# The second block of tokens lies mirrored up to the merge, so that one score matmul a level serves both blocks

## The reference

```
S_t = diag(exp(log_a_t)) S_{t-1} + k_t^T v_t
o_t = q_t S_t
# over a block, with b = cumsum(log_a) along the tokens:
scores[t, s] = sum_c q[t, c] k[s, c] exp(b[t, c] - b[s, c])   for s <= t, else 0
o = scores @ v + (q * exp(b)) @ S_before
```

## Time and profile before

| | us |
|---|---|
| median of 3 runs | 1714.46 (1712.81 to 1714.52) |
| the profiled execution | 1714.55 |
| its span, first to last instruction | 1712.8 |
| TensorE busy / weight loads | 1688.7 / 1683.3 |
| VectorE busy | 1093.8 |
| ScalarE busy | 802.7 |
| GpSimd busy | 200.8 |

### The profile page before, as it was taken

How to read it: one execution, slowest core, us unless ns; L and a number is a source line. 1 busy time by engine, 2 the same in 40 slices (tenths; PEclk the granted TensorE clock), 3 DMA queues, 4 the chain that set the end, 5 groups by cost and what they waited for, 6 DMA issues and landing times.

```text
span 1712.8 us, 37004 instructions
## 1 busy us (share of the span) xinstructions
PE 1688.7 (99%) x13836; PEld 1683.3 (98%) x13836; DVE 1093.8 (64%) x1744; ACT 802.7 (47%) x1058; POOL 200.8 (12%) x170
## 2 busy tenths in 40 slices
PE   7999999999999999999998999999999999999999
PEld 7999999999999999999998999999999999999999
DVE  6547548888888885665596544554455445555675
ACT  6575335455465444543464433543345334443453
POOL 4000001222111110005430000000000000025200
PEclk9999999999999998999998999999999999999999
DMA  9455656565665555675563555555555555555564
GB/s 261 147 195 175 219 187 199 181 200 166 186 209 189 179 175 176 225 271 186 168 193 121 190 183 173 183 192 176 181 173 185 187 181 172 179 189 184 167 191 148
DMA packets 162545, 318.66 MB, mean 186 GB/s; under 512 B 11700, under 2 KB 96436, under 8 KB 162500
## 3 DMA queue, kind: packets, MB, share of 16 engines
q1 hardware_dynamic: 160196, 315.91, 57.7%
q10 hardware_dynamic: 2304, 2.16, 0.4%
HBM read 299.94 MB, written 18.09 MB: 186 GB/s over the span
## 4 chain that ended last, share of the span: by engine, by line
PE 94%; DVE 2%; issue 2%; ACT 1%; DMA 1%; SPq 0%; POOL 0%; ACTq 0%; DVEq 0%; POOLq 0%
PE bank L291 27%; PE bank L292 26%; PE bank L293 26%; PE bank L309 3%; PE bank L311 3%; PE bank L310 3%; PE bank L583 2%; PE bank L570 1%; PE bank L559 1%; ACT whi L274 0%; DVE wlo L279 0%; PE bank L601 0%; DMA v_st<-v_spill 0%; PE bank L581 0%; PE bank L615 0%
## 5 line engine op out<-in xcount | busy, mean ns | idle before, releaser
L274 ACT CAST whi<-raw 128x1024 fp32r<-128x1024 f32 x534 | 548.3, 1048 | 469.2 <-PE bank L293 362.1
L279 DVE TENSOR_TENSOR wlo<-raw,whi 128x1024 fp32r<-128x1024 f32 x534 | 650.1, 1248 | 150.2 <-ACT whi L274 149.6
L291 PE MATMUL bank<-a_hi,whi 128*128 128x264 f32 x2576 | 737.8, 286 | 0.0
L292 PE MATMUL bank<-a_lo,whi 128*128 128x264 f32 x2576 | 730.9, 284 | 0.0
L293 PE MATMUL bank<-a_hi,wlo 128*128 128x264 f32 x2576 | 730.4, 284 | 0.0
L292 PEld LDWEIGHTS bank<-a_lo,whi 128*128 128x128 f32 x2576 | 486.7, 189 | 0.1
L291 PEld LDWEIGHTS bank<-a_hi,whi 128*128 128x128 f32 x2576 | 486.2, 189 | 0.4 <-issue 0.3
L293 PEld LDWEIGHTS bank<-a_hi,wlo 128*128 128x128 f32 x2576 | 484.1, 188 | 0.0
L291 PE MATMUL bank<-b_hi,whi 128*128 128x264 f32 x1280 | 365.4, 285 | 8.8 <-DVE wlo L279 6.7
L292 PE MATMUL bank<-b_lo,whi 128*128 128x264 f32 x1280 | 364.4, 285 | 0.0
L293 PE MATMUL bank<-b_hi,wlo 128*128 128x264 f32 x1280 | 364.2, 285 | 0.0
(11 more groups left out here) (168 smaller groups left out, 1571.5 us busy)
## 6 DMA issues: line engine op xcount, KB each, us to landing
raw<-in_stream SPq DMA_DIRECT2D x534, 512.0 KB, 4.3
m_spill<-stage SPq DMA_DIRECT2D x32, 132.0 KB, 4.7
lev<-m_spill SPq DMA_DIRECT2D x16, 264.0 KB, 5.4
S<-in_state_hgrn SPq DMA_DIRECT2D x16, 256.0 KB, 5.1
out_new_hgrn_sample<-S SPq DMA_DIRECT2D x16, 256.0 KB, 4.5
S<-in_state_gla SPq DMA_DIRECT2D x8, 512.0 KB, 7.5
out_new_gla_sample<-S SPq DMA_DIRECT2D x8, 512.0 KB, 5.6
room<-in_x SPq DMA_DIRECT2D x7, 528.0 KB, 8.0
```

Source lines behind the costliest of these rows:

```text
L274: act.copy(whi[:, s, :], raw[:, s, :]).then_inc(hi_ready, 1)
L279: dve.tensor_tensor(wlo[:, s, :], raw[:, s, :], whi[:, s, :].bitcast(F32), ALU.subtract).then_inc(lo_ready, 1)
L291: pe.matmul(out, whi[:, s, w], hi[:, k0 + k, :], start=start and k == 0, stop=False)
L292: pe.matmul(out, whi[:, s, w], lo[:, k0 + k, :], start=False, stop=False)
```

## The change

The second block's tokens (columns 128 to 255) are stored in reverse order from the very first operand on, and put back when the two branches are merged. `MIRROR` lists the three column ranges as (to, of) pairs, the middle one reversed. `a_hi` and `a_lo` are now made by three instructions each, as are the norm's reciprocal and the merge's add.

In the mirrored block a later token stands left of an earlier one. Level 0 aside, a level's query runs are the right runs of the first block and the left runs of the second, and its key runs the other way round. So 64 query columns of the one block and 64 of the other fill the 128 columns of one matmul, and 64 keys of each fill the 128 columns of `k_lev`, which needs no zeros; cells where a query of one block meets a key of the other are thrown away by the new mask `both`. GpSimd builds `both` from `masks` and `ident` with 14 copies after the start. `cells` describes such a pattern: two blocks, runs at a pitch, and the run's columns.

The sums of the second block run from its far end: a second scan, subtracting, starts at column 129, and column 128 is set to zero by GpSimd. Two small VectorE instructions form two totals a head, which GpSimd copies ahead of `cum` into two more columns of it. `kd` needs a bias for the first block only, so it is two instructions. The masking of the scores is now one instruction for levels 1 to 4 (512 columns) and one for levels 5 to 7 (384 columns).

```diff
...
+MIRROR = [(slice(0, P), slice(0, P)), (slice(P, NP_TOK), slice(NP_TOK - 1, P - 1, -1)),
+          (slice(NP_TOK, TOK), slice(NP_TOK, TOK))]
 def build(nc, t):
...
     masks = sb("masks", [P, CELLS])
+    both = sb("both", [P, LEVELS - 1, P])
     ident = sb("ident", [P, 3 * P])
...
     v_st = sb("v_st", [P, 2, TOK])
-    cum = sb("cum", [P, TOK])
+    cum = sb("cum", [P, TOK + 2])
+    totals = sb("totals", [P, 2, HEADS])
     k_b = sb("k_b", [P, TOK])
...
         pass
-    k_pad = sb("k_pad", [P, LEVELS - 1, NP_TOK])
-    probs = sb("probs", [P, 2, CELLS])
+    k_lev = sb("k_lev", [P, LEVELS - 1, P])
+    probs = sb("probs", [P, LEVELS - 1, P])
     pairs = sb("pairs", [P, 3, P])
...
     silu_done = sem("silu_done")
+    first_zero, total_ready, masks_ready = sem("first_zero"), sem("total_ready"), sem("masks_ready")
     ls_abs, ls_exp, ls_ln = sem("ls_abs"), sem("ls_exp"), sem("ls_ln")
...
-    def tokens(ap, h, side):
-        return ap.rearrange("c (p w j) -> c p w j", w=2, j=h)[:, :, side, :]
+    def cells(ap, h, at, step, pitch):
+        return bass.AP(ap.tensor, ap.offset + at, [list(ap.ap[0]), [step, 2], [pitch, 64 // h], [1, h]])
+    def rights(ap, h):
+        return cells(ap, h, h, P - h, 2 * h)
+    def lefts(ap, h):
+        return cells(ap, h, 0, P + h, 2 * h)
+    def packed(ap, h):
+        return cells(ap, h, 0, 64, h)
+    def mids(ap, h):
+        return bass.AP(ap.tensor, ap.offset + h - 1, [list(ap.ap[0]), [P + 1, 2], [2 * h, 64 // h], [0, h]])
...
                 pe.matmul(DG[:, 2 * B * P:(2 * B + 1) * P], k_b[:, at], q_b[:, at], start=True, stop=True)
-                for l in range(1, LEVELS):
-                    pe.matmul(SC[B][:, (l - 1) * 64:l * 64], k_pad[:, l - 1, at], lev[:, l, 0, B * 64:(B + 1) * 64],
-                              start=True, stop=True)
+            for l in range(1, LEVELS):
+                pe.matmul(SC[(l - 1) // 4][:, (l - 1) % 4 * P:((l - 1) % 4 + 1) * P], k_lev[:, l - 1, :], lev[:, l, 0, :],
+                          start=True, stop=True)
             pe.matmul(DG[:, P:2 * P], lev[:, 0, 1, :], lev[:, 0, 0, :], start=True, stop=True)\
...
                 act.wait_ge(x_landed[list(X_PARTS).index(k)], 16)
-            act.activation(a_hi[:, k, :], x_in[:, k, :], ACT.Identity, scale=gains[:, 0, k:k + 1]).then_inc(a_hi_ready, 1)
+            for to, of in MIRROR:
+                last = act.activation(a_hi[:, k, to], x_in[:, k, of], ACT.Identity, scale=gains[:, 0, k:k + 1])
+            last.then_inc(a_hi_ready, 1)
             round_slab(act, *wide_slab(T_RANK, k), first=k < RING)
...
             act.wait_ge(h_sem["kd_turned"], before(H))
-            act.activation(kd[:], cum[:, 0:NP_TOK], ACT.Exp, scale=-1.0, bias=cum[:, NP_TOK - 1:NP_TOK])\
-               .then_inc(h_sem["kd_exp"], 1)
+            act.activation(kd[:, 0:P], cum[:, 0:P], ACT.Exp, scale=-1.0, bias=cum[:, TOK + 1:TOK + 2])
+            act.activation(kd[:, P:NP_TOK], cum[:, P:NP_TOK], ACT.Exp, scale=-1.0).then_inc(h_sem["kd_exp"], 1)
...
         for k in range(KT):
-            gained_rest(k, a_hi, a_lo, x_in, gains[:, 0, k:k + 1], a_hi_ready, a_lo_ready)
+            dve.wait_ge(a_hi_ready, k + 1)
+            for to, of in MIRROR:
+                last = dve.scalar_tensor_tensor(out=a_lo[:, k, to], in0=x_in[:, k, of], scalar=gains[:, 0, k:k + 1],
+                                                in1=a_hi[:, k, to].bitcast(F32), op0=ALU.mult, op1=ALU.subtract)
+            last.then_inc(a_lo_ready, 1)
             rest_slab(dve, *wide_slab(T_RANK, k))
...
             dve.wait_ge(root_ready, n + 1)
-            dve.reciprocal(r_bc[:], rs[:]).then_inc(r_ready, 1)
+            for to, of in MIRROR:
+                last = dve.reciprocal(r_bc[:, to], rs[:, of])
+            last.then_inc(r_ready, 1)
             dve.wait_ge(r_ready, n + 1)
...
+            one = ones[:, 0:1].to_broadcast([P, P])
             for H in range(first, last):
-                dve.tensor_tensor_scan(gates[:, H, 0:NP_TOK], ones[:, 0:1].to_broadcast([P, NP_TOK]),
-                                       log_gate[:, H, 0:NP_TOK], 0.0, ALU.mult, ALU.add).then_inc(sums_ready, 1)
+                dve.tensor_tensor_scan(gates[:, H, 0:P], one, log_gate[:, H, 0:P], 0.0, ALU.mult, ALU.add)
+                dve.tensor_tensor_scan(gates[:, H, P + 1:NP_TOK], one[:, 1:P], log_gate[:, H, P:NP_TOK - 1], 0.0,
+                                       ALU.mult, ALU.subtract).then_inc(sums_ready, 1)
...
                 sums(8, HEADS)
+                dve.wait_ge(first_zero, 1)
+                dve.wait_ge(sums_ready, HEADS)
+                dve.tensor_tensor(totals[:, 0, :], gates[:, :, NP_TOK - 1], log_gate[:, :, NP_TOK - 1], ALU.subtract)\
+                   .then_inc(total_ready, 1)
+                dve.wait_ge(total_ready, 1)
+                dve.tensor_tensor(totals[:, 1, :], gates[:, :, P - 1], totals[:, 0, :], ALU.subtract).then_inc(total_ready, 1)
         dve.wait_ge(silu_done, 2 + HH)
...
             h = HALF[l]
-            pairs = P // h
-            left, right = tokens(cum[:, 0:NP_TOK], h, 0), tokens(cum[:, 0:NP_TOK], h, 1)
-            mid = left[:, :, h - 1:h].to_broadcast([P, pairs, h])
-            dve.tensor_tensor(lev[:, l, 0, :].rearrange("c (p j) -> c p j", j=h), right, mid, ALU.subtract)
-            return dve.tensor_tensor(lev[:, l, 1, :].rearrange("c (p j) -> c p j", j=h), mid, left, ALU.subtract)
+            if l == 0:
+                dve.tensor_tensor(lev[:, 0, 0, :], cum[:, P:NP_TOK], cum[:, TOK:TOK + 1].to_broadcast([P, P]), ALU.subtract)
+                return dve.tensor_tensor(lev[:, 0, 1, :], cum[:, P - 1:P].to_broadcast([P, P]), cum[:, 0:P], ALU.subtract)
+            dve.tensor_tensor(packed(lev[:, l, 0, :], h), rights(cum[:], h), mids(cum[:], h), ALU.subtract)
+            return dve.tensor_tensor(packed(lev[:, l, 1, :], h), mids(cum[:], h), lefts(cum[:], h), ALU.subtract)
...
         dve.wait_ge(const_landed, 16 * 6)
+        dve.wait_ge(masks_ready, 1)
...
                 h = HALF[l]
-                q, k = tokens(q_b[:, 0:NP_TOK], h, 1), tokens(k_b[:, 0:NP_TOK], h, 0)
-                lq = lev[:, l, 0, :].rearrange("c (p j) -> c p j", j=h)
-                lk = lev[:, l, 1, :].rearrange("c (p j) -> c p j", j=h)
-                dve.tensor_tensor(lq, lq, q, ALU.mult)
-                return dve.tensor_tensor(lk if l == 0 else tokens(k_pad[:, l - 1, :], h, 0), lk, k, ALU.mult)
+                if l == 0:
+                    dve.tensor_tensor(lev[:, 0, 0, :], lev[:, 0, 0, :], q_b[:, P:NP_TOK], ALU.mult)
+                    return dve.tensor_tensor(lev[:, 0, 1, :], lev[:, 0, 1, :], k_b[:, 0:P], ALU.mult)
+                lq, lk = packed(lev[:, l, 0, :], h), packed(lev[:, l, 1, :], h)
+                dve.tensor_tensor(lq, lq, rights(q_b[:], h), ALU.mult)
+                return dve.tensor_tensor(cells(k_lev[:, l - 1, :], h, 0, h, 2 * h), lk, lefts(k_b[:], h), ALU.mult)
...
             dve.wait_ge(h_sem["pv_done"], before(H))
-            for B in range(2):
-                dve.tensor_tensor(probs[:, B, :], SC[B][:, 0:CELLS], masks[:], ALU.mult).then_inc(h_sem["masked"], 1)
+            for n, (first, last) in enumerate(((0, 4), (4, LEVELS - 1))):
+                dve.tensor_tensor(probs[:, first:last, :], SC[n][:, 0:(last - first) * P].rearrange("s (l t) -> s l t", t=P),
+                                  both[:, first:last, :], ALU.mult).then_inc(h_sem["masked"], 1)
...
                 h = HALF[l]
-                to = pairs[:, 0:3:2, :].rearrange("s b (p w j) -> s b p w j", w=2, j=h)[:, :, :, 1, :]
-                cells = probs[:, :, (l - 1) * 64:l * 64].rearrange("s b (p j) -> s b p j", j=h)
+                to = cells(pairs[:, 0, :], h, h, 2 * P - h, 2 * h)
+                of = packed(probs[:, l - 1, :], h)
...
                 dve.wait_ge(h_sem["masked"], (LEVELS + 1) * H + (l + 3))
-                last = dve.tensor_tensor(to, to, cells, ALU.add)
+                last = dve.tensor_tensor(to, to, of, ALU.add)
                 last.then_inc(h_sem["probs_ready" if l == LEVELS - 1 else "masked"], 1)
...
             dve.wait_ge(tiles_drained, T + 1)
-            dve.tensor_tensor(merged[:, m, :], m_in[:, m, 0, :], m_in[:, m, 1, :], ALU.add).then_inc(merge_ready, 1)
+            for to, of in MIRROR:
+                last = dve.tensor_tensor(merged[:, m, of], m_in[:, m, 0, to], m_in[:, m, 1, to], ALU.add)
+            last.then_inc(merge_ready, 1)
...
         pool.memset(eps_col[:], EPS).then_inc(consts_set, 1)
-        pool.memset(s_feat[:], 0.0)
-        pool.memset(k_pad[:], 0.0).then_inc(consts_set, 1)
+        pool.memset(s_feat[:], 0.0).then_inc(consts_set, 1)
...
+        def side_masks(l, side):
+            h = HALF[l]
+            to = both[:, l - 1, side * 64:(side + 1) * 64].rearrange("s (p j) -> s p j", j=h)
+            if h == 1:
+                finer = ident[:, 0:P].rearrange("s (p w) -> s p w", w=2)[:, :, side:side + 1]
+            else:
```

(12 more changed lines are left out.)

## The result

The kernel with the change took 1691.56 us (median of four runs, 1690.76 to 1693.46), the kernel before, beside it, 1714.49 us (four runs, 1712.81 to 1719.91). The ratio is 0.9855, with an interval of 0.9835 to 0.9875. A second comparison, later, gave 1691.12 us (four runs, 1690.65 to 1691.70) against 1715.01 us (seven runs), 0.9853 [0.9833, 0.9873]. The forecast was 1692.2 us, in a range of 1688.5 to 1701.5.

What follows compares the result with a forecast made beforehand. The prediction took TensorE, 94% of the chain, as the bound, with VectorE's loop close behind in D=1 heads. It summed 1714.55 - 19.1 (scores) + 1.8 (D=1 heads) - 5.1 (clock) = 1692.2 us, range 1688.5 to 1701.5.

Steps and rivals of the forecast that it cites:

- The scores: TensorE's score part of each head: 20 passes of 0.110 us, 2.20 us, saving 1.59 us a head, 19.1 us over 12.
- The D=1 heads: HGRN heads, one value tile: 30.56 us each after the change, 0.26 us lost in each of 7 periods, 1.8 us.
- The account of the gaps: VectorE's gaps of 1.00 and 0.63 us in an HGRN head get used up; the loop through three engines needs 30.26 us.
- what is added to it, 0.3 us a head: Extra loop time in HGRN heads from kd's split exponential, a small GpSimd copy, and q_b and k_b copies upon VectorE's adds.
- the upper ends: Largest additions to the HGRN heads' loop, 0.8 us together, if GpSimd and VectorE lock each other out whenever they meet.
- The D=2 heads: GLA heads, two value tiles: the saved 1.59 us counts whole, since the loop goes through TensorE's scores.
- the half microsecond ahead of the scores: In GLA heads TensorE stands still 0.49 us, waiting for VectorE's new states; this wait was to stay.
- the slower rival: New patterns are slower on VectorE, 35 re-laid instructions a head, and the kernel with them: 1727 us; chance 0.06.
- Start, sums, masks, merge: Extra instructions at the start, in scans, GpSimd mask copies and the merge's add: covered by waits or idle time, nothing taken.
- The clock: The granted clock's fall in the last head, costing 5.1 us, no longer happens: -5.1 us.
- the light stretch: Last head's 0.5 us wait, narrow scores, turns and one-column work before the clock falls; 1.59 us shorter after the change.
- the rival's chance: Rival that the granted clock falls once all the same, giving 1697.3 us; chance 0.22.

## Why the prediction was right

*The scores.* Right, step by step. Predicted 2.20 us for the score part of a head, measured 2.23; predicted 1.59 us saved, measured 1.56 in a D=1 head and 1.57 in the period of a D=2 one.

*The D=1 heads.* The account of the gaps was exact but for the first head: the loop was to need 30.26 us, and it needs 30.40 - 0.14 = 30.26. The term that was mis-sized is what is added to it, 0.3 us a head. The rows show next to nothing. kd's exponential is two instructions on ScalarE (L840, L841), which overlap in part and take 0.58 us together for 0.49, less than the 0.14 more that was allowed. The small GpSimd copy took over the long time instead of adding to it, 2.15 and 0.40 us for 2.37. The adds take 2.42 us for 2.35. The mask instructions, of 512 and 384 columns, take 1.14 us for 1.16. By the sum a D=1 head was to take 30.56 us with VectorE as its bound; it takes 30.40, and TensorE is still the bound, except in the first head (30.69). TensorE's own period was put at 30.30; it saved 1.49 of the 1.56 us, the other 0.07 are spread over its matmuls, none as large as 0.05. With the 0.3 us that the first head loses, the seven periods brought 10.1 us where 9.3 were forecast, 0.8 of the 1.4 us by which the forecast fell short in the profiled execution (22.4 for 23.8). Against the median, 1691.56 us, the forecast is off by 0.6 only because that launch was the fastest of the four.

The Trainium skill, "SBUF — State Buffer", section SBUF: two separate sides, has a GpSimd instruction and a VectorE one with two SBUF inputs lock each other out for a whole instruction. The 2.15 us of a copy of two elements agree: it starts within the first of two wlo and ends with the second (334.60 and 334.56 us). The adds don't: in the D=1 head the copies of q_b and k_b, 338.97 to 339.86, lie wholly within them, and the seven adds take 2.42 us where they take 2.25 in a D=2 head that has no copy beside them. That is 0.17 us for 0.89 us of copies, far from the whole of it, so the upper ends that the prediction drew from the rule did not come about.

*The D=2 heads.* Right. The saving counts whole (36.62 to 35.06 us), the half microsecond ahead of the scores stays, and VectorE's adds end at 558.56, 1.4 us ahead of prob_v at 559.96.

*VectorE's re-laid instructions*, the mechanism of the slower rival: the two subtractions of a level have means of 282 and 281 ns (L1170 and L1171, 84 each), against 288; the multiplies have 279 and 279 ns where those of the keys had 278, and an add 309 for 302. Runs from 64 elements down to single ones, of two blocks, cost nothing, and neither does a reversed write: the merge's 32 adds of 128 columns, half of them reversed, have a mean of 288 ns, and none is over 294.

*Start, sums, masks, merge.* Nothing, as forecast. The first matmul started at 9.57 us instead of 9.36, behind a DMA that landed later, though a_lo in three pieces took VectorE up to 1.8 us where it had taken 1.0; the first head started 0.36 us sooner. The scans (eight of about 0.40 us in the last tile) with the two small ones move the next wlo from 163.60 to 163.81 us, and TensorE waits for none of it. The merge's add in three pieces takes 0.57 us for 0.43. TensorE's waits in the whole run are those of before, to 0.2 us, and the 0.24 us of the first head.

*The clock.* Right in size (4.75 us for 5.1) and in what happens, partly by luck. The step said that the light stretch is 1.59 us shorter "with as many columns in it", but the rival's chance leaned on the length alone ("the light stretch it followed is shorter"). Neither half does it by itself. With the stretch as short and half the columns the clock falls, in either kernel; with as many columns and the old length it falls too (the mirrored layout with the old passes). The chance of 0.22 for a fall would have been better bound to both. Not shown is whether the longer time or the narrower passes did it, since the two came together in every run of as many columns. That the fall is steady, which the prediction read from three runs within 1.7 us, is not so: a fourth run took 1719.91 us, of the 18 others of this kernel on one chip five lie at 1720 to 1722, and the profiles have it in different heads.

*The left 0.9 us* were no term of the sum, and come from where the clock falls within a stop that both kernels have.

## What to carry to other kernels

Count TensorE's float32 work of 64 to 128 columns in passes and not in columns: two narrow products with one stationary shape, brought into one by a layout that other engines get at no cost, save nearly a whole product. Before booking such a saving, add up the gaps of the loop behind it (here 1.63 us for 1.59), for that sum decides whether it arrives, and an engine with half a microsecond of room before has next to none after. Where the granted clock falls though TensorE is busy without a break, look at the passes that stand ahead of the fall. Here these were narrow ones with one-column ones right behind; making the narrow ones wide and fewer, or moving full ones in between, took the fall away. Either gave 5 to 6 us, and both together no more than one.

## What the runs showed of the hardware that was not expected

- A clock of 0.50 without any idle time on TensorE: behind 14 passes of 64 columns and 16 of one column, and not behind 14 of 128 and the same 16, though behind 28 of 64, as many columns in 1.51 us more, it came again. One such fall costs 4.75 to 4.78 us. Streaming half as much in the level matmuls made the kernel some 4 us slower.
- In which D=2 head it falls differs between kernels and executions, but by the windows each full one that was looked at began within a microsecond behind the first sixteen one-column passes of such a head (these end at 534.5 and 650.7 us in the mirrored layout with the old passes, at 589.4 us in the kernels of half the columns, at 643.4 us in the kernel before). There are short ones too, of some 3.4 us; those looked at began up to 0.3 us ahead of the end of these passes (575.7 for 575.96, 649.1 for 649.33). Why not in every D=2 head stays open.
- A float32 pass took 0.108, 0.111 and 0.163 us at 64, 128 and 192 columns: flat, then rising by 0.05 us for 64.
- A GpSimd copy of two elements took 2.15 us with VectorE's two wlo in the way, and the next one, of 264, 0.40 us. The other way round, 0.89 us of copies beside VectorE's adds made these 0.17 us longer.
